# Five gate projections of a delta-rule output stage, done K step by K step in earlier stages

## The reference, cut to what matters

```python
z = h @ w_in
qkv = jax.nn.silu(dw_conv(z[..., :2 * nqk + nv], conv_w))
...
gate = z[..., 2 * nqk + nv:2 * nqk + 2 * nv]
...
y = rms_norm(o, norm_g) * jax.nn.silu(gate)      # per head of 128
out = y @ w_out
```

## Time and profile before

| | |
|---|---|
| median of three runs | 3709.88 us |
| the profiled execution | 3704.88 us |
| its span in the profile | 3703.1 us |
| TensorE busy | 3559.7 us (96%) |
| VectorE busy | 1924.6 us (52%) |
| ScalarE busy | 1483.5 us (40%) |
| GpSimd busy | 866.9 us (23%) |
| HBM traffic | 81 GB/s over the span |
| mean granted TensorE clock | 0.985 of full |

### The profile page before, as it was taken

One profiled execution on the slowest core, in us unless ns is written; L12 is line 12 of the kernel. 1 busy time (PEld: TensorE's weight loads), 2 busy tenths in 40 slices (PEclk: granted clock), 3 DMA queues, 4 the chain that ended last, 5 costly groups with the idle time before them and its releaser, 6 DMA issues.

```text
span 3703.1 us, 59262 instructions
## 1 busy us (share of the span) xinstructions
PE 3559.7 (96%) x24872; PEld 2898.5 (78%) x24872; DVE 1924.6 (52%) x2927; ACT 1483.5 (40%) x2562; POOL 866.9 (23%) x844
## 2 busy tenths in 40 slices
PE   8999899999999999989999999999999799999998
PEld 5788778878887678867887888875888588878887
DVE  4667567555345657744345443447565534354343
ACT  3434334333233557644334322235674533343222
POOL 1223223212020325422200111113353221002020
PEclk8999999999999999999999999999999999999999
DMA  5011312232322122212233232220212122422222
GB/s 218 23 54 48 69 42 66 69 104 97 97 97 86 46 69 69 69 46 74 97 98 102 96 97 97 97 80 29 86 65 68 35 97 97 133 71 92 97 97 91
DMA packets 82545, 302.35 MB, mean 82 GB/s; under 512 B 8936, under 2 KB 10216, under 8 KB 81640
## 3 DMA queue, kind: packets, MB, share of 16 engines
q1 hardware_dynamic: 81248, 296.47, 24.0%
q10 hardware_dynamic: 1032, 2.10, 0.5%
HBM read 294.34 MB, written 4.19 MB: 81 GB/s over the span
## 4 chain that ended last, share of the span: by engine, by line
PE 76%; DVE 8%; ACT 6%; issue 5%; POOL 4%; DMA 0%; DVEq 0%; POOLq 0%; ACTq 0%; SPq 0%
PE ps L213 75%; DVE ac L252 1%; PE ps L218 1%; DVE wlo L244 1%; POOL p L248 1%; ACT whi L232 1%; ACT wp L233 1%; POOL u L244 1%; DVE tmp L252 0%; DVE sml L2088 0%; ACT L232 0%; ACT sg L232 0%; DVE u L244 0%; DVE ws L252 0%; DVE tmp L244 0%
## 5 line engine op out<-in xcount | busy, mean ns | idle before, releaser
L244 DVE TENSOR_TENSOR wlo<-wraw,whi 128x1024 fp32r<-128x1024 f32 x492 | 640.4, 1306 | 712.0 <-ACT whi L232 711.9
L213 PE MATMUL ps<-hh,whi 128*128 128x512 f32 x1856 | 742.1, 400 | 9.7 <-DVE ws L252 4.4
L213 PE MATMUL ps<-hl,whi 128*128 128x512 f32 x1856 | 728.7, 393 | 0.0
L213 PE MATMUL ps<-hh,wlo 128*128 128x512 f32 x1856 | 728.6, 393 | 0.0
L232 ACT ACTIVATE whi<-wraw 128x1024 fp32r<-128x1024 f32 x492 | 514.2, 1050 | 271.5 <-PE ps L213 243.2
L213 PEld LDWEIGHTS ps<-hh,whi 128*128 128x128 f32 x1856 | 351.9, 190 | 97.5 <-ACT hh L232 8.8
L213 PEld LDWEIGHTS ps<-hh,wlo 128*128 128x128 f32 x1856 | 352.1, 190 | 75.1
L213 PEld LDWEIGHTS ps<-hl,whi 128*128 128x128 f32 x1856 | 352.7, 190 | 70.1
L213 PE MATMUL ps<-u,u 64*64 64x64 f32 (+1 forms) x6016 | 224.6, 226 | 24.1 <-DVE u L244 14.8
L213 PEld LDWEIGHTS ps<-u,u 64*64 64x64 f32 x6016 | 203.7, 135 | 43.6 <-DVE u L244 17.3
L213 PE MATMUL ps<-gh,wlo 128*128 128x512 f32 x528 | 205.4, 389 | 0.0
(11 more groups left out here) (422 smaller groups left out, 6818.9 us busy)
## 6 DMA issues: line engine op xcount, KB each, us to landing
wraw<-weights SPq DMA_DIRECT2D x540, 512.0 KB, 3.3
x<-xT SPq DMA_DIRECT2D x1, 2048.0 KB, 8.6
bias_lines<-ln ACTq DMA_DIRECT2D x1, 2048.0 KB
x<-xT SPq DMA_DIRECT2D x4, 512.0 KB, 5.6
xmf<-memT SPq DMA_DIRECT2D x2, 1024.0 KB, 5.2
out<-x SPq DMA_DIRECT2D x4, 512.0 KB, 2.6
bias<-bias_lines SPq DMA_DIRECT2D x1, 1536.0 KB, 8.3
con<-consts SPq DMA_DIRECT2D x1, 1313.0 KB, 11.7
```

The costliest lines, as they stand in the source:

```text
L213: self.last, self.open = self.e.matmul(out, lhsT, rhs, start=start, stop=stop, skip_group_check=skip), True
L244: return self.e.tensor_tensor(out, a, b, op)
```

## The change

The projections of heads 1, 2, 4, 5 and 7 leave the output stage. Their 40 K steps are issued by a new `pe_early` in parts: in the first half 2, 5 and 9 steps ahead of the turns of k3, v0 and v3, and 5, 2 and 1 steps ahead of "tr", "ax" 1 and "xy" 1 of unit 0; in the second half 11 steps ahead of the turn of v3 and 5 ahead of "tr". The fillers at these turns and at "tr" go. The PSUM bank of a head is held until its eighth step is done, and until the next call of `pe_early` after it. ScalarE copies the finished gates to five SBUF tiles; sigmoid and product read these tiles. The weight blocks come in the new order, and the modulation blocks are lent at phase "ga" of unit 3 (number 27) and not at the scan's start.

```diff
+OG_EARLY = (1, 2, 4, 5, 7)
+OG_CHUNKS = ({("k", 3): 2, ("v", 0): 5, ("v", 3): 9}, {("v", 3): 11})
+OG_SCAN = ({(0, "tr"): 5, (0, ("ax", 1)): 2, (0, ("xy", 1)): 1}, {(0, "tr"): 5})
...
@@ layout
+        tiles = [W + 36416 + 512 * i for i in range(3)] + [W + 8192 + 512 * i for i in range(3)]
+        self.early = {h: self.sb("oge", o, [128, 512]) for h, o in zip(OG_EARLY, tiles)}
...
@@ pe_chunks
             elif kind != "q":
-                if (kind, i) == ("v", 3):
-                    K.pe_keep(7, "turn", hg)
+                if (kind, i) in OG_CHUNKS[hg]:
+                    K.pe_early(hg, (kind, i), OG_CHUNKS[hg][kind, i])
                 K.pe_turn6(z)
...
+    def pe_early(self, hg, place, n):
+
+        pe, x = self.pe, self.lat
+        done = self.gates[hg, place] = []
+        for h in self.og_done:
+            self.ps.drop("og", h)
+        self.og_done = []
+        for s in range(self.og_steps, self.og_steps + n):
+            h, k = OG_EARLY[s // 8], s % 8
+            if k == 0:
+                self.ps.take(pe, "og", h, hold=True)
+            b = self.ps["og", h]
+            hi, lo = self.take(self.wkey(3072 + h * 128)[k], 128)
+            pe.mm(b, hi, x.hi[k], k == 0, False)
+            pe.mm(b, hi, x.lo[k], False, False)
+            pe.mm(b, lo, x.hi[k], False, k == 7)
+            if k == 7:
+                pe.mark("og", h)
+                self.og_done.append(h)
+                done.append(h)
+        self.og_steps += n
+        self.block_of["early", hg, place] = self.blk
+
+    def act_early(self, hg, place):
+
+        act = self.act
+        for h in self.gates.get((hg, place), ()):
+            act.wait_ge(self.pe.at("og", h), self.ended("chunks", 1) if hg else None)
+            act.cp(self.early[h], self.ps["og", h]).then_inc(act("oge", h), 1)
+            act.also("ps", "og", h)
...
@@ act_chunks, step 1 of k and v
             elif kind != "q":
+                K.act_feed("early", hg, (kind, i), ahead=0)
+                if hg == 0:
+                    K.act_early(hg, (kind, i))
+                if (kind, i) == ("v", 3):
+                    for place in OG_SCAN[hg]:
+                        K.act_feed("early", hg, place, ahead=0)
...
@@ dve_chunks
+            if step and kind != "q":
+                K.dve_feed("early", hg, (kind, i), ahead=0)
+                if (kind, i) == ("v", 3):
+                    for place in OG_SCAN[hg]:
+                        K.dve_feed("early", hg, place, ahead=0)
...
@@ pe_scan
-        for g in MOD_SCANS[hg]:
-            K.lend_mod(g)
...
+            if (s, ph) in OG_SCAN[hg]:
+                K.pe_early(hg, (s, ph), OG_SCAN[hg][s, ph])
+            if (s, ph) == (3, "ga"):
+                K.pe_early(hg, (s, ph), 0)
+                for g in MOD_SCANS[hg]:
+                    K.lend_mod(g)
...
             elif ph == "tr":
-                if s == 0:
-                    K.pe_keep(3, "ramp", hg)
...
@@ act_scan
+            if hg and (s, ph) == (0, "tr"):
+                for place in OG_CHUNKS[1]:
+                    K.act_early(1, place)
+            if (s, ph) in OG_SCAN[hg]:
+                K.act_early(hg, (s, ph))
...
@@ pe_gout, act_gout, dve_gout
-            K.proj(("og", h), K.wkey(3072 + h * 128), [(K.ps.take(pe, "og", h), K.lat)])
+            if h not in OG_EARLY:
+                K.proj(("og", h), K.wkey(3072 + h * 128), [(K.ps.take(pe, "og", h), K.lat)])
...
-            act.wait_ge(K.pe.at("og", h))
-            act.a(s1, K.ps["og", h], ACT.Sigmoid).then_inc(act("osg", h), 1)
+            act.wait_ge(act.at("oge", h) if h in OG_EARLY else K.pe.at("og", h))
+            act.a(s1, K.early[h] if h in OG_EARLY else K.ps["og", h], ACT.Sigmoid).then_inc(act("osg", h), 1)
...
-            dve.tt(s1, K.ps["og", h], s1, ALU.mult).then_inc(dve("osl", h), 1)
-            dve.also("ps", "og", h)
+            dve.tt(s1, K.early[h] if h in OG_EARLY else K.ps["og", h], s1, ALU.mult).then_inc(dve("osl", h), 1)
...
@@ sync
-            if b == K.block_of["og", 7] + NRAW:
+            if b == K.block_of["og", max(h for h in ks8 if h not in OG_EARLY)] + NRAW:
                 for j in range(4):
                     K.load(f"x2_{j}", ...)
```

More of the change, by code:

```diff
@@ L401, in __init__ @@
         self.wd = self.line = None
-        self.block_of, self.nblk, self.plain, self.split, self.place_of, self.lent, self.filled = {}, 0, set(), [], {}, {}, {}
+        self.block_of, self.nblk, self.plain, self.split, self.place_of, self.lent, self.filled, self.gates = {}, 0, set(), [], {}, {}, {}, {}
         self.layout()
@@ L1323, in dve_chunks @@
                     K.dve_query_norms(hg)
-            elif kind == "k":
+            if step and kind != "q":
+                K.dve_feed("early", hg, (kind, i), ahead=0)
+                if (kind, i) == ("v", 3):
+                    for place in OG_SCAN[hg]:
+                        K.dve_feed("early", hg, place, ahead=0)
+            if step and kind == "k":
                 dve.wait_ge(K.act.at("ksq", *z, 0), K.act.at("ksq", *z, 4), dve.at("gg"), dve.at("kroot", 0) if hg else None)
@@ L1795, in dve_gout @@
             dve.wait_ge(K.act.at("osg", h))
-            dve.tt(s1, K.ps["og", h], s1, ALU.mult).then_inc(dve("osl", h), 1)
-            dve.also("ps", "og", h)
+            dve.tt(s1, K.early[h] if h in OG_EARLY else K.ps["og", h], s1, ALU.mult).then_inc(dve("osl", h), 1)
+            if h not in OG_EARLY:
+                dve.also("ps", "og", h)
             if h > 0:
@@ L3441, in tensor @@
         K.pe.begin(e)
+        K.og_steps, K.og_done = 0, []
         K.steps, K.spare = [0, 0], []
```

## The result

The changed kernel takes 3718.44 us (median of 10 runs, 3715.95 to 3720.24), the kernel before 3707.47 us beside it (10 runs, 3705.09 to 3710.72). The ratio is 1.0029, 95% interval 1.0021 to 1.0037: **slower by 11 us**. The forecast was 3711.3 us and no change. Its range of 3700 to 3721 holds the result, but by its own measure of 0.2% (7.4 us) this is "slower", to which it gave 0.16. The profiled execution took 3718.75 us, its span is 3716.9 us, at a mean granted clock of 0.981.

A forecast was written before the change was run, and what follows sets the result against it. TensorE was taken as the output stage's bound, with late conversions stopping it in the halves: +7.4 + 8.5 - 14.5 = +1.4 on 3709.88 gives 3711.3 us, no change (chance 0.70), range 3700 to 3721.

The forecast's parts named there:

- First half: Moved steps from k3's turn through the first scan's opening: late conversions and clock cost +7.4 us, ends +6 and +9.7.
- the opening's clock: First scan's opening: shift +6.1 us with kk at 2.4 GHz, +7.6 with 1.2 GHz for 3.5 us; +6.9 taken.
- The rule on transposes: v3's turn, first half: if transposes don't count as clock activity, the opening starts at 1.2 GHz and the half costs +8.1 us.
- Second half: Eleven steps wait for `wlo` until 501.5, then run partly at 1.2 GHz: +8.5 us at "tr", ends +7.9 and +10.
- I take 3.5, since the steps are dense: Second half's eleven steps: 1.2 GHz was taken to last 3.5 us after 9.5 us of idle.
- The bound of 5.3 us: Second half: the other reading of how long 1.2 GHz lasts, from 0.56 of full clock over 502 to 508.
- Output stage: Five projections fewer, the per-head chain through ScalarE and VectorE late next: -14.5 us, ends -16.3 and -13 (contention).
- the price of a head, 2.68 us: Output stage chain from one `yhi` to the next: sigmoid 0.54, product 0.63, y 0.61, `yhi` 0.90; 4.4 us with conversion.
- The half rate at the stage's end: Output stage: 1.2 GHz expected at 736 for 3.5 us after TensorE's waits, half of that lost, 1.8 us.
- Edits at nothing: Late lending of modulation blocks, bias and x loads, and held PSUM banks were expected to cost nothing.
- Rival 1: Both halves: nine and eleven steps fit the room and cost 3 us together; -11.5 us, 3698.4 us, chance 0.14.
- Rival 2: 1.2 GHz stays through a scan's opening, 7 us more per scan: 3718.3 or 3725.3, named 3720 us, chance 0.16.

The follow-up runs named there:

- experiment 1: Changed kernel with the new weight blocks ahead of v3's turn converted at step 0 of v3, not step 1, in both halves: 3698.3 us, ratio 0.9975.
- 10: Changed kernel with the conversion at step 0 of v3 in the second half only: 3705.7 us, ratio 0.9993.
- Experiment 2: Changed kernel with ten filler matmuls in TensorE's wait ahead of the second half's eleven steps: 3711.7 us, ratio 1.0012.
- experiment 5: Changed kernel with GpSimd forming the low part of y of a head only after VectorE's product for head h+2: 3715.5 us, ratio 1.0020.
- experiment 6: Kernel before with only the modulation blocks lent at phase 27 of each scan, not at its start: 3706.2 us, ratio 0.9999.

## Why the prediction was right or wrong

**The mechanism held.** TensorE waits for conversions that stand behind `sg` and `vm`, starts the scans late, and gets part of the time back in the output stage, where the head's chain takes over as the bound. The stops are 3.90 us (4.4 forecast) and 9.71 us (9.5). Experiments 1 and 10 show the cause: with the conversion one turn earlier, and nothing else, both stops go. The sum was +1.4 and the result +11, and that is sizes. The range held, but only just: 3721 is +11.1 on the forecast's scale. And the number 3711.3 looks nearer than it was. It stood on a median of three runs, 3709.88; ten runs give 3707.47. In differences the forecast is 9.6 us off, not 7.1.

**First half.** Less the 0.5 us that was there before, it is +1.3 at v2's end against +1.2, +7.7 at "tr" against +6.9, and 8.2 in all against 7.4. The difference is the opening's clock, where I had taken a middle between two. The opening ran at 1.2 GHz: its 16 "kt" matmuls took 1.12 us, as in the earlier trace rows, and half rate lasted until 197.25.

**The rule on transposes.** The opening is at 1.2 GHz behind v3's transposes and 2.4 GHz is back only in the dense steps. By the Trainium skill, TensorE: Matmul & The Clock Gate, "Part 4: PE-mode transpose", the first half would be +8.1, and the trace agrees (8.2). It doesn't prove the rule: besides the transposes only six matmuls, and another 1.77 us of idle time, stood between the stop and the opening.

**Second half.** The term that was mis-sized is "I take 3.5, since the steps are dense". The steps are dense, and 1.2 GHz lasted 6.1 us, not 3.5. The bound of 5.3 us from the earlier trace rows had been nearer, and I had set it aside. At half rate over 2.6 us more, that is 1.3 us of the 1.7 between +10.2 and +8.5. Experiment 2 bounds all of it: without the half rate the steps are 2.9 us shorter. +10.2 is 0.2 us past the end of +10.

**Output stage.** The term that was mis-sized is the price of a head, 2.68 us: I took the product (0.61) from a row in which the gate is in PSUM and priced the same instruction with both operands in SBUF alike. Beside GpSimd it takes 1.35. A head took 3.35 us from `yhi` to `yhi` without conversion, 4.47 with (4.4 forecast). Four doubled products are 4 x 0.67 = 2.7 us; experiment 5 took them away and got 2.75. Its last step of `gout 0` starts 16.3 us earlier than in the kernel before (52.36 - 36.10), the forecast's own figure. With this term alone -14.5 becomes -11.8, and -11.5 was measured. The end of -13 "by contention" was too near. The Trainium skill has the rule, in SBUF — State Buffer, "Who interferes with whom": a VectorE instruction with two SBUF inputs and a GpSimd instruction that reads SBUF exclude each other, and the one that starts first runs to its end. The trace agrees: `ylo` ends at 734.33 + 1.29 = 735.62, the product, which started while it ran, at 736.17, 0.55 us later; alone it takes 0.68.

The half rate at the stage's end came where it was forecast: 736 on the scale of the kernel before is 756.7 with the shift of 20.7, and TensorE's matmuls are slow from 754.77 on, behind a stop of 2.50 us, until 764.07. Eleven of them start from 759.52, where the last step begins, to there: 4.55 us, 2.5 at 0.23 each. That costs 2.0 us, 1.8 forecast. TensorE ran at 1.2 GHz once more (granted clock 0.57 over 740 to 744), behind the stop of 3.36 us that ends at 740.19, which costs nothing, since ScalarE takes up og 6 only at 749.66, behind other work. The stops are four, 10.2 us in all (some 11 forecast): two for a block's `wlo`, two for `ylo`, and not one per head.

One sum of the forecast is wrong: three projections are 24 steps, 16.6 us and not 8.3. It changes nothing in the -14.5, because TensorE still stood idle.

**Edits at nothing.** Right: experiment 6 for the lending; no wait for a bank shows.

**The rivals.** Rival 1, the steps hide: refuted as the change was made (the first of the eleven matmuls starts at 511.98, 9.71 us idle before), and true of the kernel of experiment 1, whose halves cost 2.6 us by the gauges and 1.4 ahead of them, 3 by the rival. It is 10.2 us faster than the kernel before beside it, 11.5 by the rival; that 3698.3 us so nearly meets the rival's 3698.4 is chance, since the two stand on different medians of the kernel before. Rival 2, 1.2 GHz through the opening: refuted, 2.4 GHz is back at 197.25 and 518.1, both before "tr". So the result lies on its side for another reason.

**The sum again**, with the measured sizes: 0.5 + 8.2 + 1.5 + 10.2 - 11.5 = +8.9, against medians 11.0 apart. The 1.5 is the stretch at 1.2 GHz in the second half's chunks, for which the sum had no term. What is left, some 2 us by the medians and 4.6 in the two profiled executions, lies behind the delta rule in places that neither kernel changes, and no run settles why. **The chances** failed in the same way: 3705 to 3719 as the forecast's own range reached into "slower by over 0.2%" (above 3717), yet I gave that side only what rival 2 had. The uncertain sizes of both halves and of the stage all came out on the dear side.

## What to carry to other kernels

When steps are moved into an idle stretch of one engine, ask first when their inputs are made: here ScalarE and VectorE convert in program order, and the place of one conversion was worth 14 us by the two gauges (20 by the medians). When a projection leaves a stage, price its next bound link by link with the operands where they will be, since an operand that goes from PSUM to SBUF can meet GpSimd on the way. And don't count steps removed as time: the projections of two late heads brought 4.4 us, those of three early ones 10.5.

## What was not expected of the hardware

- TensorE stayed at 1.2 GHz for 6.1 us of back-to-back matmuls after 9.71 us idle.
- A 128x512 product of VectorE with both operands in SBUF takes 0.68 us with GpSimd idle and 1.35 us beside GpSimd's subtraction. With one in PSUM it takes 0.68 us, but no such product ran beside `ylo`; the two instructions that form y, with one operand in PSUM, did in experiment 5, and took 0.87 us together, 0.86 without it.
- The granted clock dips or not at places whose code is the same (0.91 against 1.00 over 36 us at the second scan's end, 0.66 against 1.00 over 6 us at the first's), so gains of 1 to 2 us in one stage may show in the gauge and not in the total.
